# Expert weights laid out in 16 KB runs per partition, with strided turns of the rows; the sample tokens' combining product in four column groups

## What is computed

```
h = LN1(alpha*x + mix)
logits = h @ w_router + b_router; top 4 of 32 experts per token, gate = softmax(top 4)
for each expert e:
    u  = h[tokens of e] @ w_gu[e] + b_gu[e]          # w_gu[e]: 1024 x 2048, 8 MB
    gt = min(u[:, :1024], 7);  up = clip(u[:, 1024:], -7, 7)
    ye = ((up + 1) * gt * sigmoid(1.702*gt)) @ w_dn[e] + b_dn[e]   # w_dn[e]: 1024 x 1024, 4 MB
    y[tokens of e] += gate * ye
out = LN2(alpha*h + y)
```

## Time and profile before

| | us |
|---|---|
| median of 3 runs (1511.39 to 1520.94) | 1513.96 |
| the profiled execution | 1519.14 |
| its span, first to last instruction | 1517.3 |
| PE busy in it | 1427.2 |
| DVE, ACT, POOL busy | 433.8, 301.0, 77.8 |

### The profile page before, as it was taken

The page is one execution under the profiler, slowest core; times in us unless marked ns, Lnnn a source line. Parts: engine busy times, 40 slices in busy tenths (PEclk is TensorE's granted clock), DMA queues, the critical chain, the costliest instruction groups (busy, mean ns, idle before and its releaser), DMA issues.

```text
span 1517.3 us, 20060 instructions
## 1 busy us (share of the span) xinstructions
PE 1427.2 (94%) x7497; PEld 638.9 (42%) x7497; DVE 433.8 (29%) x885; ACT 301.0 (20%) x513; POOL 77.8 (5%) x104
## 2 busy tenths in 40 slices
PE   9898999998789999999999999999999999999994
PEld 6565656875567533333333333333332333233321
DVE  0335441264222522222132132122211221131216
ACT  1025331053231221111111111111111111111101
POOL 0202300021000000000000000000000000000000
PEclk9999999999999999999999999999999999999997
DMA  9842121253578589999999999999999999999991
GB/s 306 327 117 67 42 60 52 70 160 92 183 226 324 207 326 418 419 415 417 418 418 416 417 418 418 416 417 419 418 416 418 418 417 415 418 412 408 416 384 39
DMA packets 120022, 476.61 MB, mean 314 GB/s; under 512 B 9541, under 2 KB 39557, under 8 KB 87016
## 3 DMA queue, kind: packets, MB, share of 16 engines
q1 hardware_dynamic: 116310, 466.57, 78.1%
q0 software_dynamic: 1520, 7.41, 1.4%
q10 hardware_dynamic: 2146, 2.02, 0.4%
HBM read 471.55 MB, written 8.59 MB: 316 GB/s over the span
## 4 chain that ended last, share of the span: by engine, by line
PE 53%; SPq 28%; DMA 10%; DVE 3%; ACT 3%; issue 2%; DVEq 0%; ACTq 0%
SPq L600 25%; PE bank L1233 14%; PE bank L788 8%; PE bank L1264 7%; DMA big<-in_w_gu 6%; PE bank L1210 3%; DMA big<-in_w_in 3%; PE bank L737 2%; PE bank L958 2%; PE bank L1106 2%; PE bank L1190 2%; PE bank L1119 2%; DMA front_cols<-in_w_gu 2%; PE bank L721 1%; PE bank L1183 1%
## 5 line engine op out<-in xcount | busy, mean ns | idle before, releaser
L1233 PE MATMUL bank<-big,gates 128*64 128x512 f32 x1536 | 341.2, 595 | 18.2 <-DMA big<-in_w_gu 17.5
L1233 PEld LDWEIGHTS bank<-big,gates 128*64 128x64 f32 x1536 | 106.2, 137 | 235.7 <-issue 195.1
L2217 DVE TENSOR_TENSOR work<-work,bank 128x512 f32<-128x512 f32 x192 | 123.1, 683 | 260.3 <-PE bank L1210 260.3
L1264 PE MATMUL bank<-big,gates 128*64 128x512 f32 x768 | 170.1, 595 | 0.0
L2199 DVE TENSOR_SCALAR gates<-bank 128x512 f32<-128x512 f32 x32 | 22.1, 692 | 458.4 <-PE bank L1246 458.4
L788 PE MATMUL bank<-big 128*128 128x417 f32 (+2 forms) x384 | 115.4, 459 | 0.0
L1535 ACT ACTIVATE gates<-gates 128x512 f32<-128x512 f32 x32 | 20.2, 631 | 478.5 <-DVE gates L2199 478.5
L1210 PE MATMUL bank<-gates 64*128 64x512 f32 x396 | 111.2, 640 | 0.9 <-DVE work L2217 0.9
L1264 PEld LDWEIGHTS bank<-big,gates 128*64 128x64 f32 x768 | 53.0, 137 | 114.1 <-issue 114.1
L788 PEld LDWEIGHTS bank<-big 128*128 128x128 f32 x384 | 71.9, 189 | 39.7 <-issue 19.8
L1606 POOL TENSOR_TENSOR gates<-gates,nsaT 128x192 f32<-128x192 f32 x64 | 31.4, 512 | 1059.5 <-PE bank L1274 896.2
(11 more groups left out here) (362 smaller groups left out, 1389.4 us busy)
## 6 DMA issues: line engine op xcount, KB each, us to landing
big<-in_w_gu SPq DMA_DIRECT2D x96, 2048.0 KB, 25.8
big<-in_w_dn SPq DMA_DIRECT2D x48, 2048.0 KB, 31.3
front_rows<-in_w_gu SPq DMA_DIRECT2D x16, 2048.0 KB, 25.9
front_cols<-in_w_gu SPq DMA_DIRECT2D x16, 2048.0 KB, 23.6
front_rows<-in_w_dn SPq DMA_DIRECT2D x8, 2048.0 KB, 30.7
front_cols<-in_w_dn SPq DMA_DIRECT2D x8, 2048.0 KB, 33.2
big<-in_w_in SPq DMA_DIRECT2D x5, 2048.0 KB, 20.8
big<-in_cache_cmp_kv SPq DMA_DIRECT2D x64, 128.0 KB, 2.5
```

Of the source, the lines that this page charges most:

```text
L1233: last = pe.matmul(psum[2 + n][half * CAP:(half + 1) * CAP, :], xe[:, k % 4, (k // 4) * CAP:(k // 4 + 1) * CAP], ring_gu[slot][:, k % 2, c ...
L1264: last = pe.matmul(psum[5][half * CAP:(half + 1) * CAP, :], act_T[:, k % 4, (k // 4) * CAP:(k // 4 + 1) * CAP], ring_dn[slot][:, k % 4, ha ...
L2217: dve.tensor_tensor(y, y, psum[6 + half][:, :], ALU.add).then_inc(y_added, 1)
```

## The change

Three things, in one diff:

1. `load_piece` gives partition p consecutive rows of a piece: rows 2p and 2p+1 of a `w_gu` piece, rows 4p to 4p+3 of a `w_dn` piece. In HBM these are 16 KB in one run. So that the products still meet matching contraction rows, the transposes read their input at strides: `turn_rows` every second column of a stretch of 256, the transposes of `act_rows` every fourth of 512.
2. The t = 2 combining product becomes four products with 32 stationary columns (the real sample tokens) and 256 moving columns, each into its own 32 partitions of one bank: c = 0 and 1 from partitions 0 to 63 of `ye`, c = 2 and 3 from 64 to 127. `y_rows` of tile 2 holds the sample rows folded in the same way (four blocks of 32 partitions by 256 columns), DVE adds one 128x256 tile in place of two 128x512, and four small adds unfold it at the end. ACT starts it with four small activations in place of one.
3. Counting: five adds per expert in place of six. The t = 2 product no longer waits itself; the wait for the t = 1 adds stands before the last contraction step of line 1264.

```diff
-                sp.dma_start(dst, src.rearrange("o (a p) n -> (o p) a n", p=P)).then_inc(piece_loaded[slot], 16)
+                sp.dma_start(dst, src.rearrange("o (p a) n -> (o p) a n", p=P)).then_inc(piece_loaded[slot], 16)
...
-                    last = pe.transpose(psum[1][:, c * P:(c + 1) * P], xg[:, c * P:(c + 1) * P], ident)
+                    last = pe.transpose(psum[1][:, c * P:(c + 1) * P], xg[:, c // 2 * 256 + c % 2:c // 2 * 256 + 256:2], ident)
...
-                if bank == 6:
-                    pe.wait_ge(y_added, i * 6 + 2 * t + 6)
+                if bank == 6 and t < 2:
+                    pe.wait_ge(y_added, i * 5 + 2 * t + 5)
                 for half in range(2):
                     rows = slice(half * CAP, (half + 1) * CAP)
-                    last = pe.matmul(psum[bank + half][:, :], pgT[rows, t, :], ye[rows, :], start=True, stop=True)
+                    if t < 2:
+                        last = pe.matmul(psum[bank + half][:, :], pgT[rows, t, :], ye[rows, :], start=True, stop=True)
+                    else:
+                        for c in (2 * half, 2 * half + 1):
+                            last = pe.matmul(psum[bank][NS * c:NS * (c + 1), 0:D // 4], pgT[rows, 2, 0:NS],
+                                             ye[rows, c % 2 * (D // 4):(c % 2 + 1) * (D // 4)], start=True, stop=True,
+                                             skip_group_check=True)
...
-                    last = pe.transpose(psum[4][:, c * P:(c + 1) * P], act_rows[:, c * P:(c + 1) * P], ident)
+                    last = pe.transpose(psum[4][:, c * P:(c + 1) * P], act_rows[:, c:512:4], ident)
...
+                    if k == KD - 1:
+                        pe.wait_ge(y_added, i * 5 + 9)
...
-            for t in range(3):
+            for t in range(2):
                 act.activation(y_rows[:, t, :], h_rows[:, t, :], ACT.Copy, scale=ALPHA).then_inc(y_started, 1)
+            for c in range(4):
+                act.activation(y_rows[NS * c:NS * (c + 1), 2, 0:D // 4], h_rows[0:NS, 2, c * D // 4:(c + 1) * D // 4],
+                               ACT.Copy, scale=ALPHA).then_inc(y_started, 1)
...
-                    dve.wait_ge(y_added, i * 6 + 6)
+                    dve.wait_ge(y_added, i * 5 + 5)
+                    if t == 2:
+                        y = y_rows[:, 2, 0:D // 4]
+                        dve.tensor_tensor(y, y, psum[6][:, 0:D // 4], ALU.add).then_inc(y_added, 1)
+                        continue
...
+                    for c in range(4):
+                        own_rows = slice(NS * c, NS * (c + 1))
+                        dve.tensor_tensor(y_rows[0:NS, 2, c * D // 4:(c + 1) * D // 4], y_rows[own_rows, 2, 0:D // 4],
+                                          psum[LAST_BANKS[2]][own_rows, 0:D // 4], ALU.add).then_inc(y_added, 1)
```

More of the change, by code:

```diff
@@ L424, in trunk_kernel @@
                    "act": [(s_, 1) for s_ in (sg_ready, act_copied)],
-                   "dve": [(s_, 1) for s_ in (u_ready, ug_ready, act_ready)] + [(y_added, 6)]}
+                   "dve": [(s_, 1) for s_ in (u_ready, ug_ready, act_ready)] + [(y_added, 5)]}
         def start_counts(eng, name):
@@ L2189, in _ @@
             dve.tensor_scalar(rounds_i[:, 0:1], over[0:1, 4:5], 1.0, None, ALU.add).then_inc(place_ready, 1)
-            dve.wait_ge(y_started, 3)
+            dve.wait_ge(y_started, 6)
             start_counts(dve, "dve")
@@ L2236, in _ @@
                 if t == 0:
-                    dve.wait_ge(y_added, rounds * (6 * NE) + 6)
+                    dve.wait_ge(y_added, rounds * (5 * NE) + 5)
+                if t < 2:
+                    for half in range(2):
+                        y = y_rows[:, t, half * 512:(half + 1) * 512]
+                        dve.tensor_tensor(y, y, psum[LAST_BANKS[t] + half][:, :], ALU.add).then_inc(y_added, 1)
+                else:
+                    for c in range(4):
+                        own_rows = slice(NS * c, NS * (c + 1))
+                        dve.tensor_tensor(y_rows[0:NS, 2, c * D // 4:(c + 1) * D // 4], y_rows[own_rows, 2, 0:D // 4],
+                                          psum[LAST_BANKS[2]][own_rows, 0:D // 4], ALU.add).then_inc(y_added, 1)
                 for half in range(2):
[L2239 to L2242, removed]
+                    dve.wait_ge(y_added, rounds * (5 * NE) + 6 + (2 * t + half if t < 2 else 5 + 2 * half))
                     norm_stats(y_rows, t, half)
```

## The result

The changed kernel takes 1493.76 us (median of four runs, 1490.12 to 1498.53) beside 1516.68 us of the kernel before in the same comparison, 22.9 less: the ratio is 0.987, with a 95% interval of 0.985 to 0.989. The prediction took the 23.8 us off the 1513.96 known then; off 1516.7 it would have said 1492.9. The two profiled executions have spans of 1517.3 and 1494.6 us, 22.7 apart.

A forecast was written before the change was run, and what follows sets the result against it. The weight stream was taken to bound the kernel; 23.4 us from fewer packets plus 0.4 from the tail made 23.8 us, off the 1513.96 median: 1490 us. The forecast's own range was 1482 to 1497, at 0.70.

The forecast's parts named there:

- The bound: Expert loop: the stream of weight pieces sets the end, 30.62 us per expert where PE needs 28.82.
- the stream: Weight transfers from piece 8 to the last `w_gu` piece: 182 pieces, 23.4 us shorter after the change.
- the room: PE's slack before the last weight piece lands: 0.70 us per expert, hiding the strided loads.
- The packet price: Weight transfers: 9.6 ns per packet and engine, so 16 KB runs save 0.77 us per expert, 23.4 us in all.
- upper bound: Weight transfers: if a packet cost vanished altogether, 36 us would be saved in all.
- The late engine: Bias loads: three 4 KB packets per expert, if always on one engine, make it 0.47 us late; unchanged by the change.
- Strided transposes: Eight PE transposes per expert: strided loads cost 0 to 2.2 us, taken as a few tenths, hidden by PE's room.
- Four column groups: The t = 2 product: saves PE 0 to 0.6 us per expert, say 0.43, worth nothing in the sum.
- The moved wait: PE's wait for the tile 1 adds, before the last two of 16 products: 4.7 us of cover, costs nothing.
- The tail: After the last piece: final products some 0.6 us sooner, four small adds cost 0.1 to 0.2, net 0.4 less.

The follow-up runs named there:

- Groups alone: The kernel before with the t = 2 product in four column groups, the moved wait and five adds, weights and transposes unchanged: 1519.15 us, ratio 1.000.
- twice the bias: The changed kernel with each bias row loaded a second time into a place nobody reads: 1513.81 us, ratio 0.996 to the kernel before.
- no bias: The changed kernel with all bias rows loaded once before the loop, no bias transfer per expert: 1478.99 us, ratio 0.975 to the kernel before.
- runs only: The kernel before with 16 KB runs and strided transposes; t = 2 product, its adds and waits unchanged: 1497.69 us, ratio 0.986.

## Why the prediction was right

**The bound.** Right: the stream sets the end, the interval late in the loop is the stream's, and work for PE is free up to the room. Groups alone gained PE 0.49 us per expert and the kernel nothing. Of the 3.8 us between the forecast of 1490 and the median, 2.7 are the median of before, 1513.96 then and 1516.68 in the comparison; with the one term of weight right within 7%, little of the hit is luck.

**The packet price.** Right in kind, a little high in size. From windows of two packet sizes it said 9.6 ns; the runs say 8.4 to 9.4. A packet of 16 KB is one packet and lies on the line through 4 and 8 KB: 428 GB/s forecast and measured. The saving per expert came out at 0.72 to 0.73 us where the sum had 0.77, and the stream became 21.9 us shorter where the sum had 23.4. This term is the only one of weight, and it was 7% too large. (Its upper bound, put at 36 us, is 37 by the prediction's own figures, 128 packets of 9.6 ns over 30.3 experts.) The Trainium skill ("DMA: Bandwidth & Descriptors", "Why small descriptors are slow (HBM only)") has about 3 cycles per packet, which with its 850 MHz is 3.5 ns, an estimate. The runs measured some 9 ns, and the measurement decides.

**The late engine.** An inference of the prediction that dropped out of its difference, since confirmed in both directions: twice the bias 0.53 us more, no bias 0.54 less. It was put at 0.47; the three packets take 0.50 in the trace. What it missed is the second engine, 0.3 us late beside the first, which is why spreading the rows gained 0.14 us and not the 0.4 expected.

**Strided transposes.** It took a few tenths out of 0 to 2.2. It was 0.09 us per expert (28.91 with the runs only, 28.82 before); in the chain the transposes take 0.73 and 0.72 in place of 0.66 twice. The loads themselves did become longer, from 140 to 207 and 210 ns (changed kernel, groups by form), and are mostly covered by the transposes:

```profile
L1201 PEld LDWEIGHTS bank<-const,front_cols 128*128 128x128 f32 x132 | 18.3, 207 | 5.6 <-ACT front_cols L1534 5.6
...
L1261 PEld LDWEIGHTS bank<-const,gates 128*128 128x128 f32 x128 | 17.9, 210 | 27.4 <-DVE gates L2219 27.4
```

The steps of two (line 1201) and of four (line 1261) cost the same, so the 16-byte line of the Trainium skill ("SBUF — State Buffer", "Door 1: The DMA port swizzle"), by which only the second should miss, doesn't show.

**Four column groups.** 0.49 us saved, 0.43 assumed; the two row halves run side by side although they write one bank (0.57 us for all four, where 0.9 was put for one after the other). The PE interval of 28.42 was put at 28.39.

**The moved wait.** Nothing, as said: PE's chain runs from line 1272 into line 1214 without a pause.

**The tail.** Here the sign was wrong. PE's final products did start 0.5 us sooner after the last piece (18.99 us behind it, 19.50 before), as forecast 0.6. But the unfolding took more than the 0.1 to 0.2 allowed: from there to the end it is 21.7 us where it was 21.0 (chain of the changed kernel):

```profile
1482.86 0.40 DVE work L2260
...
1483.29 0.41 DVE work L2260
...
1483.79 0.39 issue
1484.18 0.43 DVE work L2260
```

Each small add takes 0.41 us for 32 partitions by 256, as long as the 0.42 of one for 128 partitions. Four are 1.65 us where two of 0.68 were 1.37, so the 0.35 put for one was too little; that is 0.3 of the 0.6, and the rest, in the gaps between instructions, stays open. The sum said 0.4 less, it was 0.1 more.

**What stays open.** The 0.9 us that the changed kernel's profile is ahead at the loop's start. The start of the loop moves by some us between executions and kernels (530 to 540 us), so I give it no cause. Open too: why weight packets last longer beside bias rows, and whether it is the packet or the jump of the address that costs the 9 ns.

## What to carry to other kernels

Where transfers set the pace, count packets per engine as well as bytes: two windows with different packet sizes give the price of one, and the saving follows. Read the interval between repetitions rather than the mean rate, since a piece has landed only when its last engine has: a few rows into a single partition made one engine late here by 0.53 us per expert, three quarters of what this change saved. Before a cost is put down to the packets that came in, look at the single packets: here most of it was in others. And before an engine's work is shortened, work out how long it would have to get before it binds; 0.5 us per expert was worth nothing on PE, and its room let the strided loads pass unnoticed.

## What was not expected of the hardware

- Three rows of 4 KB per expert, 0.1% of the bytes, cost 0.53 us per expert, 1.8% of the time; spread as 256-byte packets over all engines they still cost 0.40 us, of which the small packets themselves are 0.06 to 0.09.
- While bias rows arrive, two 16 KB packets of weights per expert take some 760 ns in place of 613, on another engine than that which carries the bias rows.
- A weight load at a step of two floats takes 207 ns and at four 210, against 140 contiguous.
- Products of different row halves into the same bank, on different partitions, run side by side: four of 64 rows by 32 columns with 256 moving columns in 0.57 us.
